# Reciprocal row sums of the attention blocks spread over partitions through memory, not by a transpose

## The reference, cut to what matters

```
scores = q @ k.T * hd ** -0.5        # masked or biased
p      = softmax(scores)             # exp(s - max) / row sum
out    = p @ v
```

## Time and profile before

| | us |
|---|---|
| median of 3 runs | 2954.13 (2953.7 to 2955.63) |
| the profiled execution | 2957.55 |
| its span | 2955.7 |
| PE busy | 2924.0 (99% of the span) |
| DVE busy | 1992.6 (67%) |
| ACT busy | 1232.5 (42%) |
| POOL busy | 930.5 (31%) |

### The profile page before, as it was taken

How to read it: one execution, slowest core, us unless ns; L and a number is a source line. 1 busy time by engine, 2 the same in 40 slices (tenths; PEclk the granted TensorE clock), 3 DMA queues, 4 the chain that set the end, 5 groups by cost and what they waited for, 6 DMA issues and landing times.

```text
span 2955.7 us, 50329 instructions
## 1 busy us (share of the span) xinstructions
PE 2924.0 (99%) x19328; PEld 2757.5 (93%) x19328; DVE 1992.6 (67%) x3695; ACT 1232.5 (42%) x2377; POOL 930.5 (31%) x762
## 2 busy tenths in 40 slices
PE   9999999999999999999999999999999999999998
PEld 8888887999999999999988888889999999999998
DVE  7877756388644448687878777563987444476786
ACT  5444544454322225444554444444534222255342
POOL 1211212755522226001442111137556222250013
PEclk9999999999999999999999999999999999999999
DMA  4111031333222225734521110223232222358245
GB/s 163 47 59 54 21 97 65 118 111 122 87 71 70 70 70 189 234 119 156 188 99 54 51 59 22 101 81 132 82 119 80 70 70 70 97 166 270 88 145 199
DMA packets 153451, 307.92 MB, mean 104 GB/s; under 512 B 16128, under 2 KB 76160, under 8 KB 152960
## 3 DMA queue, kind: packets, MB, share of 16 engines
q1 hardware_dynamic: 148784, 292.14, 30.2%
q10 hardware_dynamic: 4432, 12.58, 1.2%
HBM read 239.12 MB, written 57.67 MB: 100 GB/s over the span
## 4 chain that ended last, share of the span: by engine, by line
PE 89%; DVE 6%; issue 2%; POOL 1%; ACT 1%; DMA 1%; SPq 0%; ACTq 0%; DVEq 0%; POOLq 0%
PE PS L2849 27%; PE PS L2851 26%; PE PS L2850 26%; PE PS L3015 3%; PE PS L2999 3%; PE PS L2983 2%; PE PS L2971 1%; PE PS L2887 1%; POOL OSS L1400 1%; DVE ACCUM L2169 0%; PE PS L2943 0%; DVE SW L2462 0%; DVE ACCUM L2161 0%; DVE PT L2594 0%; PE PS L3024 0%
## 5 line engine op out<-in xcount | busy, mean ns | idle before, releaser
L2849 PE MATMUL PS<-XH,WH 128*128 128x512 f32 (+1 forms) x1152 | 432.9, 376 | 7.7 <-DVE VD L2440 2.8
L2851 PE MATMUL PS<-XH,WL 128*128 128x512 f32 (+1 forms) x1152 | 410.2, 356 | 0.0
L2850 PE MATMUL PS<-XL,WH 128*128 128x512 f32 (+1 forms) x1152 | 408.7, 355 | 0.0
L1428 POOL TENSOR_TENSOR GL<-GR,GH 128x512 fp32r<-128x512 f32 x186 | 251.6, 1365 | 366.4 <-ACT GH L1795 304.5
L2849 PE MATMUL PS<-DHH,DWH 128*128 128x384 f32 (+1 forms) x1056 | 328.3, 311 | 0.0
L2851 PE MATMUL PS<-DHH,DWL 128*128 128x384 f32 (+1 forms) x1056 | 326.6, 309 | 0.0
L2850 PE MATMUL PS<-DHL,DWH 128*128 128x384 f32 (+1 forms) x1056 | 325.8, 309 | 0.0
L2849 PEld LDWEIGHTS PS<-XH,WH 128*128 128x128 f32 x1152 | 217.8, 189 | 64.7 <-issue 27.1
L2851 PEld LDWEIGHTS PS<-XH,WL 128*128 128x128 f32 x1152 | 217.7, 189 | 32.7
L2850 PEld LDWEIGHTS PS<-XL,WH 128*128 128x128 f32 x1152 | 218.5, 190 | 24.5
L2850 PE MATMUL PS<-CL0T,GH 128*128 128x384 f32 x704 | 238.4, 339 | 0.0
(11 more groups left out here) (270 smaller groups left out, 8278.6 us busy)
## 6 DMA issues: line engine op xcount, KB each, us to landing
GR<-w_gu SPq DMA_DIRECT2D x62, 768.0 KB, 4.2
RAW<-w_in SPq DMA_DIRECT2D x48, 512.0 KB, 3.7
DHR<-hidden SPq DMA_DIRECT2D x66, 320.0 KB, 4.5
DWR<-w_down SPq DMA_DIRECT2D x66, 256.0 KB, 3.9
S3B<-w_down SPq DMA_DIRECT2D x66, 256.0 KB, 3.3
GR<-w_gu SPq DMA_DIRECT2D x62, 256.0 KB, 2.8
T3B<-hidden SPq DMA_DIRECT2D x44, 320.0 KB, 4.0
hidden<-S1T SPq DMA_DIRECT2D x44, 192.0 KB, 1.9
```

Of the source, the lines that this page charges most:

```text
L1428: nc.gpsimd.tensor_tensor(GL[v % 2][:, m, :, :], GR[v % 2][:, m, :, :], GH[v % 2][:, m, :, :].bitcast(F32), ALU.subtract).then_inc(s_wlo_r ...
L2849: nc.tensor.matmul(out, wh, xh, start=first, stop=False, skip_group_check=reopened)
L2850: nc.tensor.matmul(out, wh, xl, start=False, stop=False, skip_group_check=reopened)
L2851: return nc.tensor.matmul(out, wl, xh, start=False, stop=last, skip_group_check=reopened)
```

## The change

`spread_inverse` on POOL and `spread_recip` on PE go, with the tile `RC`. A small array `rates` in memory outside the core (2 buffers x 2 heads x 128) takes their place, and four tiles `RATE` of 64 rows by 128.

- ACT `send_rates(k)`: right after `across(k)`, two transfers, each of a column of `SM` (128 partitions, 4 bytes each) to `rates`.
- ACT `fetch_rates(k)`: at the head of unit 2k+3 it waits for both of them, then issues two loads, each of 128 values to 64 partitions.
- DVE `y(k)` reads `RATE` instead of PSUM, waits for `s_rate_in`, and stands behind the reciprocal of unit 2k+3 instead of at its start. For the last pair of a block it stands in the next block, behind its first two masks.
- `across(k)` now waits until `y(k-1)` has read `YS`; `values` and the turning of `v` wait for `s_summed` instead of `s_yb`.
- `store_block` and `second_biases` move from a block's end to unit 1 of the next block, ahead of that unit's copies.

```diff
         YS = place("YS", [P, 2, P], offset=base + 97984)
-        RC = place("RC", [P, 2, HD], offset=base + 99008)
+        RATE = [[place(f"RATE{n}{h}", [P, P], offset=o) for h, o in enumerate(pair)] for n, pair in
+                enumerate(((base + 99008, base + 97376), (w_at + 4 * 8192 + 3072, w_at + 4 * 8192 + 3584)))]
...
-                        if u % 2:
-                            spread_inverse(NP * (BLOCKS * L + b) + u // 2)
...
+            def send_rates(done):
+
+                a = 2 * (done % 2)
+                act.wait_ge(s_inverse, done + 1)
+                for h in range(2):
+                    act.dma_start(rates[done % 2, h, :].unsqueeze(1), SM[:, a + h:a + h + 1]).then_inc(s_rate_out, 16)
+
+            def fetch_rates(done):
+
+                act.wait_ge(s_rate_out, 32 * (done + 1))
+                for h in range(2):
+                    act.dma_start(RATE[done // NP % BLOCKS not in DIL][h][0:HD, :],
+                                  rates[done % 2, h, :].unsqueeze(0).to_broadcast([HD, P])).then_inc(s_rate_in, 16)
...
                     act.wait_ge(s_pv, NP * nb + pair + 1)
+                    act.wait_ge(s_yb, 2 * (NP * nb + pair))
...
+                if b:
+                    fetch_rates(NP * nb - 1)
                 exp(0)
                 split_v(nb, slice(4, None))
                 for u in range(NU):
+                    if b and u == 1:
+                        store_block(L, b - 1)
+                        if b - 1 == DIL[-1]:
+                            second_biases(L)
+                    if u > 1 and u % 2:
+                        fetch_rates(NP * nb + u // 2 - 1)
                     if u and u % 2 == 0:
                         across(u // 2 - 1)
+                        send_rates(NP * nb + u // 2 - 1)
...
                 across(NP - 1)
+                send_rates(NP * nb + NP - 1)
+                if b == LAST:
+                    fetch_rates(NP * nb + NP - 1)
...
                     attention(L, b, more)
-                    if b != LAST:
-                        store_block(L, b)
-                    if b == DIL[-1]:
-                        second_biases(L)
...
+            def y(L, b, pair):
+
+                done, i = NP * (BLOCKS * L + b) + pair, units_of(b)[2 * pair][0]
+                if pair == 0 and b:
+                    dve.wait_ge(s_yout, 16 * (4 * L + b))
+                dve.wait_ge(s_summed, 2 * (done + 1))
+                dve.wait_ge(s_rate_in, 32 * (done + 1))
+                for h in range(2):
+                    own = slice(HD * h, HD * h + HD)
+                    rate, total = RATE[b not in DIL][h][0:HD, :], YS[0:HD, h, :]
...
+                    nc.vector.tensor_tensor(to[own], rate, total, ALU.mult).then_inc(s_yb, 1)
...
                 mask(0)
                 mask(1)
+                if b:
+                    y(L, b - 1, NP - 1)
...
-                    if u > 1 and u % 2:
-                        y(u // 2 - 1)
...
                         nc.vector.reciprocal(SM[:, a:a + 2], SM[:, a:a + 2]).then_inc(s_inverse, 1)
+                    if u > 1 and u % 2:
+                        y(L, b, u // 2 - 1)
                     with_unit(u)
                 add_parts(NP - 1)
-                y(NP - 1)
+                if b == LAST:
+                    y(L, b, NP - 1)
...
-                        pe.wait_ge(s_yb, 2 * (NP * nb + pair))
+                        pe.wait_ge(s_summed, 2 * (NP * nb + pair))
...
-                def spread_recip(pair):
-
-                    pe.wait_ge(s_recip, NP * nb + pair + 1)
-                    pe.wait_ge(s_summed, 2 * (NP * nb + pair + 1))
-                    nc.tensor.transpose(PS[:, Y_BANK, 0:P], RC[:, :, :].rearrange("p h d -> p (h d)"), ident) \
-                        .then_inc(s_rb, 1)
...
                 if b not in DIL:
-                    pe.wait_ge(s_yb, 2 * NP * nb)
+                    pe.wait_ge(s_summed, 2 * NP * nb)
                     turn_v(nb, slice(4, None))
...
-                    if u and u % 2 == 0:
-                        spread_recip(u // 2 - 1)
...
-                spread_recip(NP - 1)
...
+    rates = nc.dram_tensor("rates", [2, 2, P], F32, kind="Internal").ap()
```

More of the change, by code:

```diff
@@ L498, in build @@
 def build(nc, xt, w_in, w_out, w_gu, w_down, gains, conv_w, bias, tables, small, mixed,
-          parked, hidden, out):
+          parked, hidden, rates, out):
     with ExitStack() as ctx:
@@ L678, in build @@
         s_inverse = sem("inverse")
-        s_recip = sem("recip")
+        s_rate_out = sem("rate_out")
+        s_rate_in = sem("rate_in")
         s_across = sem("across")
         s_summed = sem("summed")
-        s_rb = sem("rb")
         s_yb = sem("yb")
@@ L1474, in scale_taps @@
                         .then_inc(s_scaled_y, SCALED_Y.step((L, j, c)))
[L1476 to L1483, removed]
             def mixed_low(L, c, m):
@@ L2511, in split_v @@
                                             ALU.subtract).then_inc(s_vl, 1)
+            def y(L, b, pair):
[7 more added lines that the diff above has]
+                    rate, total = RATE[b not in DIL][h][0:HD, :], YS[0:HD, h, :]
+                    if b not in DIL and i < 8:
+                        to = queries(YB, i)
+                        rate, total = (t.rearrange("p (r c) -> p r c", c=Q_COLS) for t in (rate, total))
+                    else:
+                        to = stepped(YB, *half_of(i)) if b in DIL and i < 8 else YB[:, i * P:(i + 1) * P]
+                    nc.vector.tensor_tensor(to[own], rate, total, ALU.mult).then_inc(s_yb, 1)
             def attention(L, b, table, with_unit, last_cover):
@@ L3324 @@
     hidden = nc.dram_tensor("hidden", [FT, P, T], F32, kind="Internal").ap()
+    rates = nc.dram_tensor("rates", [2, 2, P], F32, kind="Internal").ap()
     out = nc.dram_tensor("out", [P, KT, T], F32, kind="ExternalOutput").ap()
-    build(nc, *args, mixed, parked, hidden, out)
+    build(nc, *args, mixed, parked, hidden, rates, out)
     r = run_bass_kernel_spmd(nc, [arrays], core_ids=[0])
```

## The result

| | before | after |
|---|---|---|
| median, 4 runs each | 2954.88 us (2953.7 to 2959.03) | 3554.48 us (3552.18 to 3557.64) |
| ratio | | 1.2022, 95% interval 1.2006 to 1.2037 |
| span of the profiled execution | 2955.7 | 3555.8 |

The change costs 600 us. The forecast was 2967 with a range of 2941 to 3002: the sign was right, the size was not.

What follows compares the result with a forecast made beforehand. The prediction took PE, busy for 99% of the span, as the bound. It summed -13.9 (PE work and waits), +13.8 (loop), +8.6 (moved parts) and +4 (queue disturbances) to +12.5, so 2967 us, range 2941 to 3002.

Steps and rivals of the forecast that it cites:

- Landing of a send ... Taken: 1.9: In each pair, a column's store from issue to landing: 1.9 us, between 1.7 and 3.4, the latter from the taps.
- Taken: 2.2: In each pair, a fetch of the rates from issue to landing: 2.2 us, between 1.9 and 3.4.
- the forecast's own loop: From one across to the next through send, fetch, y and YS: 5.8 us, 6.1 with allowance; 13.8 us in two layers.
- landings over 3 us: Sign that the prediction is wrong: sends or fetches landing later than this; expected 1.7 to 2.2 and 1.9 to 2.6.
- The rival of slow 4-byte stores: In each pair, a read on top of a send's write, 1.9 us more: loop 8.0 us, about 3011, chance 0.13.
- The steps from one across to the next are ...: Between across starts: first send's issue, second send's landing, first fetch's issue, second fetch's landing, two multiplications, four hand-overs; 5.8 us.
- the same delay of the same pairs: ACT's four issues a pair, 1.9 us, delay the short pairs' copies as the loop does; not added, 0 to 2 us a layer.
- Blocks 0 to 2: nothing, their pairs are longer.: In blocks 0 to 2 the loop from pair to pair costs nothing, since their pairs are longer than it.
- 100 transposes by 0.11 us = 11.0 us: Transposes removed from PE, 0.11 us each, all on the path: 11.0 us gained, 13.9 with PE's waits for y.
- Two multiplications are moved on DVE, none is added: 0: On DVE, the two multiplications of y only change place, at a cost of 0.
- What is moved: store_block and second_biases ahead of unit 1's copies: in block 3 PE loses 4.3 us, 8.6 in two layers, bounds 0 to 16.
- The sends behind the bias loads: At block 3's start, pair 0's sends queue behind bias loads and land at about 401, not 398; PE loses some 2.5 us.

Runs made afterwards that it cites:

- e4: The changed kernel with the rates kept inside the core: sends write to rows of spare partitions of YS, fetches spread them over 64 partitions; 3077.18 us.
- e2: The changed kernel with the 4-byte pieces of a send 64 bytes apart in memory, fetches from a constant row; 3032.37 us.
- e3: The changed kernel with the 4-byte pieces of a send 512 bytes apart in memory, fetches from a constant row; 3031.93 us.
- e12: The changed kernel with the 4-byte pieces of a send 32 bytes apart in memory, fetches from a constant row; 3042.18 us.
- e11: The changed kernel with sends of only 16 adjacent 4-byte pieces instead of 128, fetches from a constant row; 3039.7 us.
- e14: The changed kernel with its sends unchanged, but fetches taking a constant row instead of the row just written; 3543.49 us.
- e16: The changed kernel with adjacent sends and constant-row fetches, ACT waiting only for the sends of two pairs back; 3275.76 us.
- e1: The changed kernel with each send storing one contiguous row of 512 bytes instead of a column of 4-byte pieces; 3007.74 us.
- e13: The kernel before without its 100 transposes and copies, y still reading an operand from PSUM, division left out; ratio 0.9964, 2947.21 us.
- e10: The kernel before without its 100 transposes and copies, constant rates fetched once a block, waits as in the changed kernel; ratio 0.9992.
- e7: The changed kernel without sends, with two fetches of a constant row in every pair; ratio 1.0108 against before.
- e8: The changed kernel with two sends of a contiguous row in every pair and constant rows fetched once a block; ratio 1.0068 against before.
- e5: The kernel before with only store_block and second_biases moved to unit 1 of the next block; ratio 1.0008.
- e6: The changed kernel without sends and with constant rows fetched once a block, division left out; ratio 1.0031 against before.

## Why the prediction was wrong

**"Landing of a send ... Taken: 1.9", with 3.4 as the upper bound.** This is the step that failed. On the chain of after it measured 6.7 to 16.8 us, with a median of 8.1. The fetch, "Taken: 2.2" with the same upper bound, has a median of 3.5 to landing. Put into the forecast's own loop, with the issues measured, they give 0.41 + 8.1 + 0.45 + 3.5 + 0.6 + 0.2 = 13.3 us instead of 6.1, and 2 x 9 x (5 x 13.3 - 9.6 - 9.7 - 8.4 - 7.0 - 5.6) = 472 us instead of 13.8. The forecast's sum is then +467 of the 600 us, without the slower clock. So it was built rightly in the main, and one term sank it. The forecast had named the sign: landings over 3 us. The bound came from the taps, the only narrow transfer in the trace, but that is a load, and its pieces land in the core's memory. e4 shows that there narrow pieces are harmless (2.0). A bound may only be taken from a row with the same direction and the same memory; for an adjacent narrow store the trace held none, so the upper end was open and I closed it.

**The rival of slow 4-byte stores** named the right place and had 0.13, at 3011. Its price, one more read of 1.9 us, was the wrong kind: a cost for each transfer. (The shortest landing in the earlier trace rows is moreover 1.7, a store's; 1.9 is the shortest load's.) The measured cost grows with the density of the pieces: from 64 bytes apart to 512 the landing stays at 1.5. The Trainium skill (DMA: Bandwidth & Descriptors, section Specifications) says that pieces under 512 B are read, modified and written. The direction agrees, but all of e2, e3, e12 and e11 have such pieces too and land in 1.4 to 1.6 us, so the rule as stated doesn't tell the dear case from the cheap ones.

**"The steps from one across to the next are ..."** The loop through fetch, `y` and `YS` is real: `across` waits for `y` in 62 pairs of after. It is one of two ways. ACT, which issues the fetch, waits for the send in its own program, ahead of the copy for `values`. I had this queue before me ("the fetches, issued once the sends have landed at about 2.4") and set it aside as "the same delay of the same pairs". With a slow landing that is nearly so: the way through ACT binds in the other pairs, and 90 copies stand 667 us behind the sends. PE itself meets the loss there: 341 us of its idle time end with the low part for `values`. 268 us of the loss (e14 less e16) go with ACT's wait, for both ways together.

**"Blocks 0 to 2: nothing, their pairs are longer."** True of a loop of 5.8 us, and still true in e1 and e2 (9.5, 9.7 to 9.9, 8.4). It failed with the landing.

**"100 transposes by 0.11 us = 11.0 us".** PE's side was right: e13 gives -10.5 us. In the kernel as changed it came to -1.8 (e10), because of "Two multiplications are moved on DVE, none is added: 0". Their form changed, from one operand in PSUM to both in the core's memory. The trace of before had a sign of the price; two more of its groups (min/median/max ns), the first with both operands in the core's memory, the second with one:

```profile
L2464 DVE TENSOR_TENSOR Rk<-Rk,TAB x18: 416/680/2614, 41.9 to 1688.0; 128x512 f32<-128x512 f32 x12, 128x256 f32<-128x256 f32 x6
...
L2445 DVE TENSOR_TENSOR TA<-PS,RS x18: 419/690/692, 62.2 to 1940.4; 128x512 f32<-128x512 f32 x12, 128x256 f32<-128x256 f32 x6
```

The same median, but only the first has a maximum of 2.6 us, about one L1390 of POOL. The Trainium skill (SBUF — State Buffer, section Who interferes with whom) says that a VectorE instruction with two operands there contends with a GpSimd instruction that reads there, and that one with at most one such operand doesn't, outside the modes that use both ports. The runs agree with both halves: the two multiplications take 3.22 us beside POOL in e10, and 0.80 in e13, also beside POOL.

**"This is the same delay of the same pairs as the loop's, so I don't add it"**, on ACT's issues. This was mis-sized: e7 and e8, which have no round trip, cost 24.6 and 11.8 us, together 18 us a layer where I had bounds of 0 to 2; the 22 waits are in that.

**"What is moved" held in kind.** PE at the start of block 3 was to be 1.8 us late; 1.7 measured (e5). The sends behind the bias loads were to cost 2.5 us a layer; with a fetch in their place the second `across` came 3.6 us late (e6). In time, e5 is 1.6 us over before by the medians and not distinguishable from no change.

**The clock** isn't in the prediction. PE was hardly ever idle before (32 us), the granted clock in its attention blocks was 1.00, and I took lost time as idle time alone; 183 us came as slower work.

What the quick version costs, as a sum of differences between medians: -10.5 (PE work, e13), +8.7 (`y`'s operands, e10), +10.9 (moved parts and `y`, e6), +24.6 (fetches, e7), +11.8 (row sends, e8) = +45.5, near the +51 of e1, in which they also wait for each other. No version here with this change that divides beats before, and there is little to win: taking the transposes and copies out altogether gives 10.5 us of 2958 (e13).

## What to carry to other kernels

A column of 4-byte values stored into adjacent words of outside memory may land five times as late as the same values spread 32 bytes or more apart; if a small round trip is wanted at all, look at the landing of exactly that shape, direction and memory first, and treat a missing row as an open end. A wait put ahead of a transfer's issue holds every later instruction of the issuing engine: list these beside those that need the data. And when an operand moves from PSUM to the core's memory, the instruction is another one: look in the trace for the maximum, not the median, of VectorE operations with two such operands beside GpSimd.

## What the runs showed of the hardware that was not expected

- 128 adjacent 4-byte stores to outside memory: a median of 8.1 us from issue to completion (6.7 to 16.8, after), the packets gone within about 1.5 us. 3.0 at 8 bytes apart, 1.6 at 32, 1.5 at 64 and 512, 1.4 for 16 adjacent ones, 2.0 inside the core. Its mechanism is open. Transfers issued behind them on the same queue land late (e16: 7.8 us instead of 2.7), and loads on SP's queue too (after: 6.8 instead of 3.7).
- The granted clock was 0.50 for products that came after 3.11 us of idle PE, in a stretch of such gaps (after), and was 0.74 over blocks 3 and 4; from 830 us on, with PE busy, it was 0.99.
- Issuing a 4-byte column takes ACT 0.41 us (0.32 to 0.95), a broadcast fetch 0.55 (up to 1.66); 200 fetches, with 12 waits for them, cost 24.6 us (e7 less e6).
- Copying one partition's row to 64 partitions inside the core lands in 3.5 us (e4), slower than from outside memory (2.5, e1).
- A VectorE multiplication of 64x128 with both operands in the core's memory takes up to 2.59 us beside GpSimd and at most 0.39 otherwise (e10); with one in PSUM at most 0.41 in either case (e13).
